# A streaming encoder trunk on one core: sample state products in pairs of PSUM banks, output blocks one place sooner, and steps of the turns, exponentials, residual and sample keys moved

## What is computed

```python
zxbcdt = u @ w_in                                   # z, x, B, C, dt
xbc, new_buf = causal_conv(xbc, conv_buf, conv_w, conv_b); xbc = silu(xbc)
dt = softplus(dt_raw + dt_bias); A = -exp(A_log)
# per chunk: y = (C B^T * decay) x + (C s) * exp(acs);  s = s * exp(acs_end) + B^T (x * to_end)
y = rmsnorm((y + Dp * xs) * silu(z), norm_g)
return y @ w_out, new_buf, s_new
```

## Time and profile before

| | |
|---|---|
| median of 3 runs | 1864.04 us (1861.62 to 1868.81) |
| the profiled execution | 1858.17 us, span 1856.4 us |
| mixer, from its first block to the FFN behind it | 290 to 600 us of the span |
| sample attention | 1397 to 1494 us |

### The profile page before, as it was taken

The page is one execution under the profiler, slowest core; times in us unless marked ns, Lnnn a source line. Parts: engine busy times, 40 slices in busy tenths (PEclk is TensorE's granted clock), DMA queues, the critical chain, the costliest instruction groups (busy, mean ns, idle before and its releaser), DMA issues.

```text
span 1856.4 us, 28263 instructions
## 1 busy us (share of the span) xinstructions
PE 1811.9 (98%) x10561; PEld 1732.7 (93%) x10561; DVE 1134.6 (61%) x1708; ACT 827.4 (45%) x1424; POOL 231.7 (12%) x286
## 2 busy tenths in 40 slices
PE   9999999999999999999999999999998999999997
PEld 8999999799888999999999999986777899999997
DVE  6545446979889654544874544456777755545444
ACT  5333335665464433333553333346665544333232
POOL 1000010311311000011400001132012130000110
PEclk9999999999999999999999999999999999999999
DMA  6344444456352644444344444440225534444441
GB/s 209 123 126 129 143 137 149 154 204 232 121 203 86 198 118 134 122 140 140 116 141 134 122 126 144 140 154 30 56 73 147 158 114 144 117 131 125 143 141 57
DMA packets 67652, 249.74 MB, mean 135 GB/s; under 512 B 8312, under 2 KB 9592, under 8 KB 66288
## 3 DMA queue, kind: packets, MB, share of 16 engines
q1 hardware_dynamic: 57584, 205.32, 36.4%
q0 software_dynamic: 9984, 43.27, 7.0%
HBM read 235.77 MB, written 12.12 MB: 134 GB/s over the span
## 4 chain that ended last, share of the span: by engine, by line
PE 83%; DVE 10%; ACT 2%; DMA 2%; issue 1%; POOL 1%; SPq 0%; DVEq 0%; POOLq 0%; ACTq 0%
PE pair L1862 23%; PE pair L1864 23%; PE pair L1863 23%; DVE wlo L1224 2%; PE pair L2272 2%; PE pair L2273 2%; PE pair L2274 2%; PE pair L2363 1%; DVE cy L1352 1%; DVE S L1448 1%; DMA lowA<-in_cacheT 1%; DMA raw<-in_stream 1%; DMA wv<-in_wv 1%; PE pair L1869 0%; PE pair L1871 0%
## 5 line engine op out<-in xcount | busy, mean ns | idle before, releaser
L1862 PE MATMUL pair<-xh,whi 128*128 128x384 f32 x1928 | 649.8, 337 | 4.4 <-DVE xl L1234 3.9
L1864 PE MATMUL pair<-xh,wlo 128*128 128x384 f32 x1928 | 644.5, 334 | 0.0
L1863 PE MATMUL pair<-xl,whi 128*128 128x384 f32 x1928 | 644.4, 334 | 0.0
L1224 DVE TENSOR_TENSOR wlo<-raw,whi 128x1024 fp32r<-128x1024 f32 (+3 forms) x372 | 465.2, 1252 | 174.7 <-ACT whi L701 166.0
L701 ACT ACTIVATE whi<-raw 128x1024 fp32r<-128x1024 f32 (+2 forms) x369 | 378.4, 1029 | 272.2 <-PE pair L1864 258.9
L1862 PEld LDWEIGHTS pair<-xh,whi 128*128 128x128 f32 x1928 | 361.9, 188 | 11.2 <-issue 4.8
L1863 PEld LDWEIGHTS pair<-xl,whi 128*128 128x128 f32 x1928 | 362.0, 188 | 1.6 <-issue 1.0
L1864 PEld LDWEIGHTS pair<-xh,wlo 128*128 128x128 f32 x1928 | 361.9, 188 | 0.0
L1244 DVE TENSOR_TENSOR tg<-pair,rstd 128x384 f32<-128x384 f32 x88 | 49.1, 558 | 328.0 <-PE pair L1864 327.3
L1862 PE MATMUL pair<-ah,whi 128*128 128x384 f32 x704 | 236.6, 336 | 0.0
L1864 PE MATMUL pair<-ah,wlo 128*128 128x384 f32 x704 | 236.6, 336 | 0.0
(11 more groups left out here) (398 smaller groups left out, 2243.9 us busy)
## 6 DMA issues: line engine op xcount, KB each, us to landing
raw<-in_stream SPq DMA_DIRECT2D x372, 512.0 KB, 3.7
S<-in_ssm POOLq DMA_DIRECT2D x4, 2048.0 KB, 8.9
out_ssm_s<-S POOLq DMA_DIRECT2D x4, 2048.0 KB, 7.8
seg<-acs_rows POOLq DMA_DIRECT2D x12, 512.0 KB, 6.0
cTb<-in_cacheT POOLq DMA_DIRECT2D x10, 512.0 KB, 4.1
kn<-rs_rows SPq DMA_DIRECT2D x16, 264.0 KB
lowC<-in_cache SPq DMA_DIRECT2D x8, 512.0 KB, 3.2
lowA<-in_cacheT POOLq DMA_DIRECT2D x6, 512.0 KB, 5.9
```

Source lines behind the costliest of these rows:

```text
L1224: V.tensor_tensor(wlo[:, r, 0:w], raw[:, r, 0:w], whi[:, r, 0:w].bitcast(F32), ALU.subtract).then_inc(lo_ready, 1)
L1862: M(out, whi[:, r, ws], mh_(k), start=first and k == k0, stop=False)
L1863: M(out, whi[:, r, ws], ml_(k), start=False, stop=False)
L1864: ins = M(out, wlo[:, r, ws], mh_(k), start=False, stop=last and k == k1 - 1)
```

## The change

The sample products are issued as four sets of two, in banks 4 and 5 (the fourth set in banks 0 and 3; in the last group in 4 and 5, 6 and 7, 4 and 7, 5 and 6). PE now runs: y tile 1, set 0, y tile 2, set 1, in0 of the next group, set 2, in1, set 3, out0, in2, out1, in3, in4, out2 and so on. The turns take x first, then B, then C by B. In group 0 the exponentials go behind the scaling of in5. The last output block's earlier sum is added to h ahead of its product. In the sample attention the split of keys is parted from that of rope keys; the first is moved into the last unit of the past sums, the second goes ahead of the turns' use, and the turned norms of streams 6 and 7 come one unit later, on POOL behind the loads of stream 2.

```diff
-        order += [("in", g, 0), ("in", g, 1), ("in", g, 2), ("out", g - 1, 0), ("in", g, 3), ("out", g - 1, 1), ("in", g, 4)]
+        order += [("in", g, 0), ("in", g, 1), ("out", g - 1, 0), ("in", g, 2), ("out", g - 1, 1), ("in", g, 3), ("in", g, 4)]
...
         def state_bank(g, i):
-            return bank[(6, 7, 4, 5, 4, 7, 5, 6)[i] if g == GROUPS - 1 else (6, 7, 4, 5, 4, 5, 0, 3)[i]]
+            r = i // 2
+            if g == GROUPS - 1:
+                return bank[(4, 5, 6, 7, 4, 7, 5, 6)[i]]
+            return bank[3 * (i % 2) if r == 3 else 4 + i % 2]
...
-            pool.wait_ge(rs_ev, 3)
-            pool.dma_start(rs_past(6, 8, 0, 3 * P), rsT[0:2 * MH, :]).then_inc(rs_st, 16)
-            pool.dma_start(rs_past(6, 8, 3 * P, P), rsT2[0:2 * MH, 0:P]).then_inc(rs_st, 16)
             for b in range(2, STREAMS):
                 past_keys(b)
                 past_rope(b)
+                if b == 2:
+                    pool.wait_ge(rs_ev, 3)
...
+                if b == 5 and g == 0:
+                    act.preload_act_table(ACT.Exp)
+                    decay_rows()
                 if b < 6:
                     ch = channels(g, b)
...
+                if b == 5 and g == 0:
+                    decay_exps()
+                    act.preload_act_table(ACT.Silu)
                 if 1 <= b <= 6 and (g or 1 < b < 6):
                     silu(g, b - 1)
...
                 if g:
+                    out_proj(g - 1, 0)
                     for i in range(4):
                         y_square(g - 1, i)
                 in_proj(g, 2)
...
                 if y + 1 < MH // 2:
                     p_exp(2 * y + 3)
                 else:
+                    keys_split(0)
                     act.wait_ge(rs_turn_ps, 2)
...
                 s_turned(u)
+                if u % 2 and u // 2 + 2 < STREAMS:
+                    rope_split(u // 2 + 2)
+                if u == 1:
+                    act.wait_ge(rs_turn_ps, 3)
...
+                dve.wait_ge(conv_done, 6 * g + 6)
                 dve.wait_ge(filled, 3)
                 V.tensor_copy(bass.AP(Cm, 0, ...
...
+            def residual_part(b):
+                two = slice(2 * b, 2 * b + 2)
+                dve.wait_ge(f_evac, 8 * (GROUPS - 1))
+                step(V.tensor_tensor(facc[:, two, :], facc[:, two, :], bc(rstd[:, 0, :], (P, 2, TOK), 1), ALU.mult))
+                step(V.tensor_tensor(h[:, two, :], h[:, two, :], facc[:, two, :], ALU.add))
...
+                if b < 3:
+                    dve.wait_ge(f_evac, 8 * (GROUPS - 1) + 2 * b + 2)
+                    src = facc[:, two, :]
+                else:
+                    dve.wait_ge(blk, CRED + out_block(GROUPS - 1, b) + 1)
+                    src = f_pair(GROUPS - 1, b)
...
                 if g:
                     in_proj(g, 0)
-                    evac(g, 1)
-                    state_add(g - 1, 2)
-                    conv(g, 1)
+                    in_proj(g, 1)
                     state_add(g - 1, 3)
+                    out_proj(g - 1, 0)
...
                 state_add(g, 1)
                 y_rows(g)
+                if not last:
+                    state_add(g, 2)
...
+                if b == 0:
+                    residual_part(3)
...
                     past_sums(8 * y + i)
+                    if i == 4 and not more:
+                        keys_split(0)
...
             def turns(g):
-                pe.wait_ge(conv_done, 6 * g + 6)
+                pe.wait_ge(conv_done, 6 * g + 4)
...
+            def sample_states(g, r):
+                if r == 0:
                     pe.wait_ge(yo_ready, 2 * g + 2)
                     pe.wait_ge(s1_ready, 2 * g + 2)
+                elif r == 1 and g == GROUPS - 1:
+                    pe.wait_ge(in_evac, 10 * GROUPS)
+                elif g == GROUPS - 1:
+                    pe.wait_ge(state_ready, 8 * g + 4)
+                elif r < 3:
+                    pe.wait_ge(state_ready, 8 * g + 2 * r)
                 else:
+                    pe.wait_ge(y_evac, 4 * g + 4)
+                for i in (2 * r, 2 * r + 1):
+                    j, e = i % 4, i // 4
                     rows32 = slice(32 * j, 32 * j + 32)
+                    ins = M(state_bank(g, i)[:, :], Bm[rows32, e, :], xw[rows32, 2, :], start=True, stop=True)
                 ins.then_inc(state_ps, 1)
...
                 in_proj(g, 0)
+                if g:
+                    sample_states(g - 1, 2)
                 in_proj(g, 1)
...
                 if g:
-                    sample_states(g - 1, 1)
+                    sample_states(g - 1, 3)
+                    out_proj(g - 1, 0)
...
-                if u == 0:
+                if u == 1:
                     pe.wait_ge(past_rstd, 4)
                     rs_turn(bank[1], 6, 8)
```

More of the change, by code:

```diff
@@ L1094, in _, with keys_split @@
             p_exp(1)
+            def keys_split(b):
+                s = b % 2
+                act.wait_ge(c_ld[s], 16 * (STREAMS // 2 + b // 2 + 1))
+                if b >= 2:
+                    act.wait_ge(sc_ps, 2 * b - 2)
+                A(cTh[:, s, :, 0:PAST], craw if b >= 2 else cTb[:, s, :, 0:PAST], ACT.Copy)
+                A(cTh[:, s, :, PAST:KEYS], cT[:, :, SEQ + STEPS * b:SEQ + STEPS * b + STEPS], ACT.Copy).then_inc(past_hi, 1)
             value_evac(3)
@@ L1174, in _ @@
             keys_split(1)
[L1175 to L1178, removed]
+            rope_split(1)
             for u in range(UNITS):
@@ L1745, in _, with keys_split @@
             p_norm(1)
+            def keys_split(b):
+                s = b % 2
+                new = slice(SEQ + STEPS * b, SEQ + STEPS * b + STEPS)
+                dve.wait_ge(past_hi, STREAMS + b + 1)
+                V.tensor_tensor(cTl[:, s, :, 0:PAST], craw if b >= 2 else cTb[:, s, :, 0:PAST], cTh[:, s, :, 0:PAST].bitcast(F32),
+                                ALU.subtract)
+                V.tensor_tensor(cTl[:, s, :, PAST:KEYS], cT[:, :, new], cTh[:, s, :, PAST:KEYS].bitcast(F32),
+                                ALU.subtract).then_inc(past_lo, 1)
             past_split(1)
@@ L1824, in _ @@
                     keys_split(1)
+                    rope_split(1)
+                elif u % 2 == 0 and u // 2 + 1 < STREAMS:
+                    rope_split(u // 2 + 1)
                 if u + 1 < UNITS:
                     s_max(u + 1)
+                if u == 0:
+                    dve.wait_ge(past_std, 2)
+                    V.reciprocal(ksq[:, :, 6:8], ksq[:, :, 6:8]).then_inc(past_rstd, 1)
                 if u % 2 and u // 2 + 2 < STREAMS:
@@ L2010, in turns @@
             def turns(g):
-                pe.wait_ge(conv_done, 6 * g + 6)
+                pe.wait_ge(conv_done, 6 * g + 4)
                 if g:
                     pe.wait_ge(state_ready, 8 * g)
-                for t in range(TT):
-                    ins = nc.tensor.transpose(bank[3][:, tiles(t)], BC[:, 0, tiles(t)], ident[:, :])
-                ins.then_inc(bt_ps, 1)
-                if g:
-                    pe.wait_ge(f_evac, 8 * g - (4 if g == GROUPS - 1 else 0))
                 else:
@@ L2022, in turns @@
                 for t in range(TT):
-                    ins = M(bank[5][:, tiles(t)], BC[:, 0, tiles(t)], BC[:, 1, tiles(t)], start=True, stop=True)
-                ins.then_inc(g_ps, 1)
-                for t in range(TT):
                     for i in range(4):
@@ L2028, in turns @@
                     ins.then_inc(xt_ps, 1)
+                pe.wait_ge(conv_done, 6 * g + 5)
+                for t in range(TT):
+                    ins = nc.tensor.transpose(bank[3][:, tiles(t)], BC[:, 0, tiles(t)], ident[:, :])
+                ins.then_inc(bt_ps, 1)
+                pe.wait_ge(conv_done, 6 * g + 6)
+                if g:
+                    pe.wait_ge(f_evac, 8 * g - (4 if g == GROUPS - 1 else 0))
+                for t in range(TT):
+                    ins = M(bank[5][:, tiles(t)], BC[:, 0, tiles(t)], BC[:, 1, tiles(t)], start=True, stop=True)
+                ins.then_inc(g_ps, 1)
             def first_states(g):
@@ L2110, in _ @@
                 in_proj(g, 9)
-                y_tile(g, 1)
-                sample_states(g, 0)
-                y_tile(g, 2)
+                if last:
+                    sample_states(g, 0)
+                    y_tile(g, 1)
+                    sample_states(g, 1)
+                    y_tile(g, 2)
+                    sample_states(g, 2)
+                else:
+                    y_tile(g, 1)
+                    sample_states(g, 0)
+                    y_tile(g, 2)
+                    sample_states(g, 1)
             out_proj(GROUPS - 2, 2)
```

69 lines of the change are left out of this document (22 added, 47 removed).

## The result

| | before | changed |
|---|---|---|
| median of 12 runs | 1863.05 us (1859.98 to 1868.81) | 1868.55 us (1865.53 to 1870.89) |
| ratio to before (95% interval) | | 1.0029 (1.0020 to 1.0037) |
| profiled execution, its span | 1858.17, 1856.4 us | 1867.84, 1866.0 us |

The changed kernel is 5.5 us slower by the medians, 0.3%: the interval excludes "equal" and stays within the 0.5% that the prediction counted as no change. The range held it; the forecast of 1864.2 is 4.35 us too low.

What follows compares the result with a forecast made beforehand. PE was taken as the bound, working 1811.9 of 1856.4 us. The terms 0.0 + 2.2 + 1.55 - 0.5 - 3.0 = +0.2 us, put on the median of 1864.0, gave 1864.2 us; range 1857 to 1872.

Steps and rivals of the forecast that it cites:

- rival 2: Passage between groups: VectorE becomes the bound; 1 us late at each of three passages gives 1867.2 us; chance 0.14.
- Pairs, 1.07 us each: Sample products: a set of two holds PE 1.07 us, like a set of four; 8 more sets add 8.6 us.
- Passage 1 to 2 costs +2.2: Passage from group 1 to group 2: six blocks end 2.2 us later, with PE waiting 0.5 us at out1.
- No further wait follows: the later f_adds end 0.5 us or more ahead of PE: Passage 1 to 2, behind out1: DVE's later adds that free banks for output blocks never make PE wait.
- 0.0 for group 0 and this passage together: Group 0 and passage 0 to 1: sooner turns cancel the third pair and 0.45 us waiting at out1, total 0.0.
- 1.7 to 2.1 us later: Group 0: the moved exponentials and the three decay-row DMAs after them come 1.7 to 2.1 us later.
- Last group and passage 2 to 3, +1.55: Passage 2.2, minus 1.3 as x turns cover the wait for C, plus 0.65 at out block 2: +1.55 us.
- Residual, -0.5: Last output block: adding its earlier sum to h beforehand takes 0.5 us off the 1.6 us wait for xl.
- Attention, -3.0: Sample attention: moved splits and turned rows shorten waits by 3.0 us, with ends -1.5 and -5.0.
- Rival 1: Sample attention: the transfer of keys stays the bound, -1.5 in place of -3.0, or 1865.7 us; chance 0.22.

Runs made afterwards that it cites:

- e4: The changed kernel with VectorE's squares' sum put ahead of input block 3 of the next group: 1865.55 us, ratio 1.0030 to the kernel before.
- e7: The changed kernel with the output blocks back in their old places, pairs kept: 1860.79 us, ratio 0.9990 to the kernel before.
- e1: The kernel before with the attention part of the change alone: 1859.34 us beside 1861.37, ratio 0.9990.
- e2: The kernel before with only x's turns ahead of B and C and the exponentials moved: 1860.83 us beside 1861.37, ratio 1.0008.
- e3: The changed kernel with sets of four and the output blocks in their old places: 1857.23 us, ratio 0.9975 to the kernel before.
- e10: e4 timed once more, beside e9: 1866.24 us, ratio 1.0017 to the kernel before.
- e6: e5 with the copy of the decay rows also ahead of the load of the Exp table: 1850.60 us, ratio 0.9942 to the kernel before.
- e9: The changed kernel as it is, timed again: 1868.33 us beside 1862.68 for the kernel before, ratio 1.0032.
- e5: e3 with the decay rows stored as soon as ScalarE has copied them: 1853.43 us beside 1862.89, ratio 0.9948 to the kernel before.
- e11: The changed kernel with the edits of e4, e5 and e6 together: 1860.44 us beside 1862.68, ratio 0.9984 to the kernel before.
- e8: The kernel before with only stream 0's key split ahead of the last past sums: single execution, attention stretch 95.27 us.
- e12: The kernel before with the decay rows stored as soon as they are copied, nothing else changed: 1866.58 us in a single execution.

## Why the prediction was right or wrong

The verdict, no change within 0.5%, was right and the range held, but the likeliest case did not happen. Nearest to what happened is rival 2, which had 0.14: DVE late in the passage, with 1867.2 us at 1 us for each passage. The other part, the decay rows that come late in group 0, stood in no rival.

- *Pairs, 1.07 us each*: right, 1.06.
- *"Passage 1 to 2 costs +2.2"*: 3.74. The 0.5 us at out1 came as 0.46. The step that failed is "No further wait follows: the later f_adds end 0.5 us or more ahead of PE". I followed DVE and PE as far as out1 and took the margin behind it as given; the squares' sums had moved relative to in3 and in4, and out3 waited 1.44. e4 shows that those sums made 1.0 us of it, e7 that the rest goes with the old order.
- *"0.0 for group 0 and this passage together"*: 5.5 us in the profiles (88.1 to 93.5 from the decay sums to the turns of group 1), 3.8 against e1 (89.7). The turns ended 0.6 us sooner than I said. The step that failed is the term "1.7 to 2.1 us later" for the exponentials' three DMAs: ACT had its first decay rows 3.9 us later (329.93 to 333.85), of which the exponentials account for 1.3, the landing of the store for 1.7 and that of the load for 0.9. Counted from the decay sums, which PE reached 0.44 us sooner, it is 4.4 us, and the store was issued 1.7 later: the issue came as forecast, the landings did not. I carried a landing time over from the old place as if it were a constant. With it the lead was gone; a stretch at half the clock (1.6 us), the pairs, 0.46 and 0.79 us at out1 and out3 were paid in full.
- *Last group and passage 2 to 3, +1.55*: 2.84. x covers the wait for C, as said, only with the old passage (e2, e3); with the late DVE a wait of 1.44 us stays there (0.42 in e10).
- *Residual, -0.5*: -0.72 (1.6 us for xl became 0.87), and 1.66 to 0.77 from e2 to e3.
- *Attention, -3.0*: -4.1 in the profiles, within the ends; the first values product came 3.7 us sooner as forecast. Rival 1 did not happen.

Sum of the profiles: 5.5 + 3.7 + 2.8 - 0.7 - 4.1 = 7.2 us in the places named, where I had 0.2. 1.6 of it is the lower clock that the profile of before was spared (last section). That the verdict came out right is luck: a loss of 10 to 12 us in the mixer and a gain of 4 in the attention left 5.5 by the medians, inside the 9.3 that counted as no change.

## What to carry to other kernels

Where a wait is taken out, the next input of the same engine must be followed back to its own source, DMAs included, at the new time and in the new order; a landing time read in the old place is one sample. When a block moves by one place, walk the other engines' lists to the end of the passage: small work that sat in a gap may come to lie on the chain. And read a small difference by stretches and by parts undone: here a change that measured as 0.3% slower held some 10 us of loss, and with its passage undone and the decay rows sooner it is 11 us faster than before (e6).

## What the runs showed of the hardware

**TensorE's clock fell behind a wait of 3 us.** The granted clock of windows in group 0 of the changed kernel (columns: PE, PEld, DVE, ACT, POOL busy, clock, DMA share, GB/s):

```profile
338.90:341.90 3.00, 0.04 (x1) 0.00 (x0) 2.25 (x3) 3.00 (x9) 3.00 (x3) 1.00 0.00 0
343.90:347.30 3.40, 3.40 (x22) 3.07 (x21) 3.37 (x6) 3.37 (x10) 0.00 (x0) 0.50 0.36 95
347.40:351.00 3.60, 3.60 (x24) 3.54 (x22) 1.11 (x2) 3.57 (x6) 1.51 (x2) 1.00 0.73 255
```

0.50 is the lower of its two levels (1.2 of 2.4 GHz). All seven profiles with the 3.0 us wait at the old state (changed, e2, e3, e4, e7, e9, e10) show such a stretch there, the three without it (e5, e6, e11) none. Its length differs: 3.4 us above, while in e10 the clock read 0.50 from 344 to 349 us. Behind the 3.4 us wait at the turns it stands in e1, e8 and e12, but not in the profile of before, which therefore was 1.6 us quicker there than theirs (88.1 against 89.5 to 89.7 us from the decay sums to the turns of group 1):

```profile
328.00:331.40 3.40, 3.25 (x27) 3.26 (x28) 2.30 (x5) 2.51 (x7) 0.00 (x0) 1.00 1.01 347
```

```profile
328.00:331.40 3.40, 3.40 (x18) 3.40 (x17) 2.81 (x6) 2.88 (x9) 0.00 (x0) 0.50 1.03 349
```

(The first is before, the second e1.) A place that no edit touches, near 1230 us, had no such stretch in before and 10.2 us of it in e12:

```profile
1225.10:1235.30 10.20, 8.81 (x30) 7.71 (x30) 4.98 (x13) 2.37 (x5) 0.00 (x0) 0.50 0.19 53
```

The long stretch took 805.9 us there, against 800.9 before, and 803.0 and 800.9 in the two profiles of the changed kernel, so two profiled executions can differ by 5 us without a cause in the change.

**POOL waited 1.6 to 4.5 us for the landing of the same 48 KB store.** It was 1.74 us in before, 1.62 in e1, 1.58 in e5, 1.79 in e6, 1.59 in e8 and 1.93 in e11; 3.44 in the changed kernel, 3.89, 3.67 and 3.42 in e2 to e4, 3.56, 3.68 and 3.53 in e7, e9 and e10, and 4.54 in e12. From issue to landing that is 1.8 to 2.2 us for the short ones and 3.7 to 4.8 for the long. In slices of 0.4 us the long ones were issued within about half a us after the DMA engines had taken up a weight block, the others in a pause or about 1 us into a block. The Trainium skill, page "DMA: Bandwidth & Descriptors", section "Anatomy of one DMA — SWDGE (gpsimd) path", gives a DMA a fixed cost of about 2.0 us whatever its size; the short ones agree, the long ones do not. That the weight block is the cause was not tried by itself and stays open.
